# Sums of squares per attention head: two rounded passes of a high and a low part in place of full-precision matmuls, in a two-layer decoder step on one Trainium2 core

## The reference, cut to what matters

```python
def _rms_norm(x, g):
    xf = x.astype(jnp.float32)
    y = xf * lax.rsqrt(jnp.mean(xf * xf, axis=-1, keepdims=True) + EPS) * g.astype(jnp.float32)
    return y.astype(x.dtype)
...
            z = h @ p["w_in_att"][j]
...
            q = _rope(_rms_norm(q, p["q_norm_att"][j]), pos)
            k = _rope(_rms_norm(k, p["k_norm_att"][j]), pos)
...
        qx = _rms_norm(qx.reshape(n, t, N_X_HEADS, HEAD_DIM), p["q_norm_x"][i])
```

## Time and profile before

| what | value |
|---|---|
| median of 3 runs | 1170.79 us (1170.48, 1170.79, 1173.45) |
| profiled execution, span from first to last instruction | 1172.9 us |
| TensorE busy | 1145.8 us (98%) |
| VectorE busy | 804.7 us (69%) |
| ScalarE busy | 522.0 us (45%) |
| GpSimd busy | 132.1 us (11%) |
| mean granted TensorE clock | 0.995 |

### The profile page before, as it was taken

One profiled execution on the slowest core, in us unless ns is written; L12 is line 12 of the kernel. 1 busy time (PEld: TensorE's weight loads), 2 busy tenths in 40 slices (PEclk: granted clock), 3 DMA queues, 4 the chain that ended last, 5 costly groups with the idle time before them and its releaser, 6 DMA issues.

```text
span 1172.9 us, 22169 instructions
## 1 busy us (share of the span) xinstructions
PE 1145.8 (98%) x8990; PEld 1105.8 (94%) x8990; DVE 804.7 (69%) x1201; ACT 522.0 (45%) x901; POOL 132.1 (11%) x140
## 2 busy tenths in 40 slices
PE   5999999999999999999999999999999999999998
PEld 5999665999999999999999999999999999999998
DVE  6789965798668558568658545689866855856853
ACT  7633767357227326326423222436722722732630
POOL 0038743000000000000241121200000000000000
PEclk9999989999999999999999999999999999999999
DMA  8553150213223312313522321221321332231231
GB/s 330 186 162 116 51 180 1 74 71 115 102 73 106 112 58 87 141 36 108 189 98 73 144 75 70 75 97 48 124 96 70 109 108 69 82 136 38 105 136 48
DMA packets 23146, 120.18 MB, mean 102 GB/s; under 512 B 2708, under 2 KB 6932, under 8 KB 9892
## 3 DMA queue, kind: packets, MB, share of 16 engines
q1 hardware_dynamic: 17892, 100.93, 24.6%
q0 software_dynamic: 1632, 10.54, 2.5%
q10 hardware_dynamic: 3552, 7.74, 1.9%
HBM read 111.29 MB, written 5.69 MB: 100 GB/s over the span
## 4 chain that ended last, share of the span: by engine, by line
PE 82%; DVE 8%; ACT 4%; DMA 2%; issue 2%; POOL 2%; ACTq 1%; DVEq 0%; SPq 0%; POOLq 0%
PE zps L498 44%; PE zps L757 23%; PE zps L745 4%; PE ops L757 4%; DVE tmp L969 2%; PE ops L672 1%; DVE w_lo L907 1%; PE tps L642 1%; POOL sm L1856 1%; PE zps L549 1%; DVE sm L1037 1%; ACT xf L1377 1%; ACT w_hi L1377 1%; DMA tmp<-z 1%; PE zps L596 1%
## 5 line engine op out<-in xcount | busy, mean ns | idle before, releaser
L498 PE MATMUL zps<-act_hi,w_hi 128*128 128x272 f32 x1664 | 348.6, 291 | 0.9 <-DVE w_lo L907 0.9
L498 PE MATMUL zps<-act_hi,w_lo 128*128 128x272 f32 x1664 | 344.1, 288 | 0.0
L498 PE MATMUL zps<-act_lo,w_hi 128*128 128x272 f32 x1664 | 343.2, 288 | 0.0
L757 PE MATMUL zps<-xf,wf 128*128 128x272 f32 x2304 | 299.2, 290 | 2.3 <-ACT tmp L1377 1.3
L757 PEld LDWEIGHTS zps<-xf,wf 128*128 128x128 f32 x2304 | 294.3, 188 | 3.2 <-issue 1.5
L498 PEld LDWEIGHTS zps<-act_hi,w_hi 128*128 128x128 f32 x1664 | 262.1, 188 | 5.4 <-issue 2.9
L498 PEld LDWEIGHTS zps<-act_lo,w_hi 128*128 128x128 f32 x1664 | 261.5, 189 | 0.0
L498 PEld LDWEIGHTS zps<-act_hi,w_lo 128*128 128x128 f32 x1664 | 259.9, 189 | 0.0
L1377 ACT ACTIVATE w_hi<-w_stage 128x2048 fp32r<-128x2048 f32 (+1 forms) x61 | 114.8, 1883 | 150.9 <-PE zps L498 123.6
L907 DVE TENSOR_TENSOR w_lo<-w_stage,w_hi 128x2048 fp32r<-128x2048 f32 x59 | 137.5, 2331 | 43.6 <-ACT w_hi L1377 43.4
L1377 ACT ACTIVATE wf<-w_sum 128x1024 fp32r<-128x1024 f32 x64 | 67.9, 1061 | 195.8 <-DVE w_sum L925 88.2
(11 more groups left out here) (182 smaller groups left out, 1291.9 us busy)
## 6 DMA issues: line engine op xcount, KB each, us to landing
w_stage<-wst SPq DMA_DIRECT2D x92, 1024.0 KB, 4.9
kx<-xkT POOLq DMA_DIRECT2D x4, 1024.0 KB, 6.3
vx<-xv POOLq DMA_DIRECT2D x4, 1024.0 KB, 7.1
x_res<-xT ACTq DMA_DIRECT2D x2, 1088.0 KB, 7.6
tmp<-z ACTq DMA_DIRECT2D x32, 68.0 KB, 2.1
yT<-x_res ACTq DMA_DIRECT2D x7, 272.0 KB, 2.0
memx<-memT SPq DMA_DIRECT2D x2, 512.0 KB, 4.8
vb<-swav POOLq DMA_DIRECT2D x1, 1024.0 KB, 8.6
```

Source lines behind the costliest of these rows:

```text
L498: mm = pe.matmul(zps[slot][:, h, 0:n], w_[:, d, k, w:w + 128], r_[:, k, c0 + h * n:c0 + (h + 1) * n], start=(j == 0 and i == 0), stop=(j = ...
L757: mm = pe.matmul(bank, wf_hl[pw][:, fw, a, :], x_form(l, px, fx, a)[:, 0, :], start=(begin and a == 0 and j == 0), stop=(a == KC // 2 - 1 ...
```

## The change

For head blocks n = 0 to 9 (`N_QX[1]` is 10), `headsum` no longer multiplies the squares in float32. ScalarE copies the squares, rounded, to a new tile `sq_hi`, directly behind the square and with a wait for it; VectorE subtracts to get `sq_lo`, as the last step of its iteration i, for block i; TensorE waits for `n_lo` and runs for each half two rounded matmuls, with a rounded copy `head_r` of `headones`, which ScalarE makes once near the start.

```diff
@@ place
+    sq_hi, _ = place("sq_hi", [128, 2, NT], f32r, at=at_act[1] + 12 * NT * 4)
+    sq_lo, _ = place("sq_lo", [128, 2, NT], f32r, at=at_act[1] + 14 * NT * 4)
...
+    head_r, _ = place("head_r", [128, 128], f32r)
@@ headsum(n), TensorE
+                if n < N_QX[1]:
+                    pe.wait_ge(h_rdy, 1)
+                    pe.wait_ge(n_lo, n + 1)
+                    take(tfree)
+                    for h in range(2):
+                        c = slice(h * HALF, (h + 1) * HALF)
+                        pe.matmul(tps[:, h, 0:HALF], head_r[:, :], sq_hi[:, n % 2, c], start=True, stop=False)
+                        mm = pe.matmul(tps[:, h, 0:HALF], head_r[:, :], sq_lo[:, n % 2, c], start=False, stop=True)
+                    mm.then_inc(n_ms, 1)
+                    tfree[0] = (n_sd, n + 1)
+                    return
                 pe.wait_ge(n_sq, n + 1)
@@ VectorE
+            def square_lo(n):
+                dve.wait_ge(n_hi, n + 1)
+                dve.tensor_tensor(sq_lo[:, n % 2, :], tmp[:, n % 2, :], sq_hi[:, n % 2, :].bitcast(f32), ALU.subtract).then_inc(n_lo, 1)
...
                 if 1 <= i <= 10:
                     head_norm(i - 1)
+                if i < 10:
+                    square_lo(i)
@@ square(n), ScalarE
                 act.activation(tmp[:, n % 2, :], norm_src(n), ACT.Square).then_inc(n_sq, 1)
+                if n < N_QX[1]:
+                    act.wait_ge(n_sq, n + 1)
+                    copy(sq_hi[:, n % 2, :], tmp[:, n % 2, :]).then_inc(n_hi, 1)
...
             split_hi(0, 1, first=True)
+            copy(head_r[:, :], headones).then_inc(h_rdy, 1)
```

More of the change, by code:

```diff
@@ L170, in build_kernel @@
         n_sq, n_ms, n_sd, n_out = (sem("n_" + s) for s in ("sq", "ms", "sd", "out"))
+        h_rdy, n_hi, n_lo = sem("h_rdy"), sem("n_hi"), sem("n_lo")
         r_sw, r_out = [sem(f"r_sw{i}") for i in range(2)], sem("r_out")
```

## The result

The changed kernel takes 1185.59 us (median of 4 runs, 1185.04 to 1186.81) against 1172.12 us of the kernel before on the same chip (4 runs): ratio 1.0108, 95% interval 1.0089 to 1.0126, so it is **slower by 12.7 us** (0.0108 x 1172.1; the interval makes it 10.4 to 14.8; the two medians lie 13.5 apart, inside it). The forecast was 1190.4 us, 19.6 us slower, with a range of 1177 to 1195.

The account below looks back on a forecast made before the run. The prediction took TensorE to bound the stage, VectorE close behind. VectorE's additions (6.9 us) and waiting for GpSimd (12.4) made `z(11)` 19.3 us later; 0.3 behind gave 19.6, so 1170.8 + 19.6 = 1190.4 us, range 1177 to 1195.

Parts of the forecast that it names:

- TensorE's saving of 4.3 us: Attention projection: ten head sums at 0.50 instead of 0.93 us save 4.3 us, but all is lost in waiting.
- the bound of the stage is TensorE: Attention projection's twelve panels, kernel before: TensorE has work in all 78.00 us, with VectorE close behind.
- The sum without GpSimd: VectorE's iterations with copy and subtraction: odd 7.67 us, even 7.77, iteration 10 8.2; `z(11)` 6.9 us later.
- The exclusive pair: VectorE and GpSimd exclude each other for whole instructions; GpSimd gets between scaling and subtraction, costing 0 to 1.3 us each.
- Rival 2: GpSimd does not get in between scaling and subtraction: `z(11)` near 137.4, total 1180 us; chance 0.24.
- the first case: Likeliest case: VectorE's additions plus waiting for GpSimd in the stage give 1190 us, range 1186 to 1194; chance 0.62.
- the 12.4 us of waiting for GpSimd: VectorE's waits for the shared pair: 8.9 us in iterations 5 to 8, 3.5 in iterations 3 and 4.
- rotation starts at `z`+5.5: GpSimd's rotation of a block starts 5.5 us after VectorE's panel read, as the swapped copy is issued 0.68 later.
- Iteration 9: GpSimd stands still in iteration 9, as its last block waits for head sum 9, so no waiting is counted there.
- Weight transfers are asked for later, and needed later by the same amount.: Weight transfers shift together with the chain behind the stage; no time was added for them.
- Rival 3: TensorE's granted clock falls to half while it stands still in iterations: 15.5 us more, 1206; chance 0.06.
- Behind the stage: After `z(11)`: GpSimd's late work serves the first probabilities in part, adding 0.3 us; everything after shifts as a whole.

Follow-up runs that it names:

- runs 1: Changed kernel with the head sums put back to two float32 matmuls behind the same waits: 1185.8 us, 1.0123 of the kernel before.
- run 2: TensorE's part alone against the kernel before: square written rounded, four rounded matmuls, no copy, no subtraction; 1173.8 us, ratio 1.0012.
- run 3: GpSimd's rotation cut from 544 to 8 columns in both kernels: changed 1178.8 us (1.0050), before 1172.2 us (0.9985).
- run 6: VectorE's reciprocal cut from 544 to 8 columns in both kernels: changed 1172.4 us (0.9993), before 1171.9 us (0.9996).
- run 4: The stage's weight transfers cut from 1024 to 128 KB in both kernels: changed 1191.1 us (1.0157), before 1174.5 us (1.0012).
- the kernel with the root first: Changed kernel with ScalarE's rounded copy moved behind the square root, rotation kept: 1186.2 us, 1.0126 of the kernel before.

## Why the prediction was right, and where it was off

- *The side, and the bound.* Right for the changed kernel: TensorE's saving of 4.3 us was lost in waiting (runs 1 and 2), VectorE is the bound, and the stage alone carries the loss. For the kernel before, "the bound of the stage is TensorE" was too much said. VectorE waited for a panel last at `z(4)`, and no engine relieved alone gave more than 1.3 us of stage: TensorE nothing (run 2), GpSimd's rotation 1.3 (run 3), VectorE's reciprocal 1.3 (run 6).
- *The sum without GpSimd.* Right to 0.1 us per iteration: 7.66 and 7.75 against 7.67 and 7.77; block 0 2.78 against 2.67; iteration 10 8.03 against 8.2.
- *The exclusive pair.* Right, and now shown for two instructions in a row: GpSimd gets in between, and the subtraction takes 1.84 to 1.87 us in iterations 3, 5 and 7, where 0.72 is its own time, so 1.1 us of each is waiting. The rule of the Trainium skill (page "SBUF — State Buffer", section "SBUF: two separate sides"), one instruction holds the pair and the other blocks, agrees with these rows and with the run without rotation. Rival 2 has fallen.
- *The number.* 1185.6 us lies in the stated range and just below the 1186 to 1194 of the first case by itself. The stage grew by 13.5 us, not 19.3.
- *The term that was mis-sized* is the 12.4 us of waiting for GpSimd. It measured 6.5: scalings 1.6, subtractions 3.4, low parts of weights 1.6. The step that failed is "rotation starts at `z`+5.5" for even iterations. There it started at `z`+9.1 to 9.8 (odd ones: 5.5 to 5.6), because the rounded copy pushed the transfers of the swapped block 0.7 us later, into those of the weights. Rotations then came in pairs, and even iterations met only the last operation. The run with short weights takes this away: both instructions then wait in even iterations too, 11.1 us in all. The mechanism was right, its phase was not.
- *Iteration 9.* The forecast has GpSimd stand still in it. It rotated block 6 there, from 126.51 to 130.64, and was done before the scaling at 131.96, so this cost nothing.
- *"Weight transfers are asked for later, and needed later by the same amount."* True of their own landing, and blind to what they share the DMA engines with. That sentence is where I should have looked.
- *Rival 3.* The clock did fall, in iterations 5 and 8, for part of a panel each. The wait before the next head sum covered it but for 0.1 to 0.2 us: `z(9)` started 0.13 us after VectorE was ready. In other runs it was not covered whole (0.74 us at `z(10)` of run 4, 1.44 in the kernel with the root first), so the price of this rival changes from case to case.
- *Behind the stage* the trace is 2.3 us shorter than before (1042.1 against 1044.4 from `z(11)` to the end), where I had added 0.3. Of that, 0.85 lie between `z(11)` and the output projection (71.25 us to its start at 212.58, against 72.10 to 200.64), where the granted clock was a little higher in this profile (0.83 against 0.79 in the 20 us with the lowest); the rest I have not traced. Runs of the kernel before spread over more than that.

## What to carry to other kernels

An engine that reads 98% busy may have another one right behind it; before taking work off it, look how late that one runs, and count what the change gives it. A step put at the end of a dependent chain that goes round three engines can cost its own time even where its engine is idle for longer than that elsewhere in the chain: the subtraction cost 0.6 us behind the scaling and nothing inside VectorE's 2.02 us of waiting for the root (7.66 against 7.06 us per odd iteration, without rotation). And where two engines exclude each other, the loss depends on when they meet: get the phase from every queue that feeds them, transfers of other things included, before multiplying one meeting by the number of iterations.

## What the runs showed of the hardware that I had not expected

- Four transfers of 68 KB took 8.2 us from the first issue with 1024 KB of weights asked for 2.0 us behind them (7.6 and 7.8 in iterations 4 and 8), and 3.9 us with the weights asked for 2.7 us behind, or not at all. Slower transfers made the changed kernel faster: with less to transfer it lost 5.5 us.
- The granted clock fell to half for a few microseconds at a time in a stage where TensorE worked 73.63 of 87.30 us, after stops of at most 2.50 us; in the kernel before, with work throughout, it stayed at 1.00 in the window of the earlier trace rows.
- A VectorE subtraction that follows a scaling 0.08 us before that one's record ends still lets a waiting GpSimd operation in between: 1.85 us instead of 0.72.
